# Two chained norms between the blocks: both sums from one pass, and fused norm bodies

## The reference

```python
h = h + swiglu(rmsnorm(h, norm2_w[layer]), w_ffn_in[layer], w_ffn_out[layer])
return rmsnorm(h, final_norm_w)
```

```python
h_l = rms_norm(x_lat, g_norm_mix[i]) * (1.0 + sc1_l) + sh1_l
```

## Time and profile before

| what | value |
|---|---|
| median of 3 runs | 3028.16 us (3027.71 to 3032.05) |
| the profiled execution | 3027.03 us, its span 3025.2 us |
| TensorE busy | 2884.8 us, 95% |
| VectorE, ScalarE, GpSimd busy | 1829.3, 1187.3, 305.2 us |
| mean granted TensorE clock | 0.984 of full speed |

### The profile page before, as it was taken

The page is one execution under the profiler, slowest core; times in us unless marked ns, Lnnn a source line. Parts: engine busy times, 40 slices in busy tenths (PEclk is TensorE's granted clock), DMA queues, the critical chain, the costliest instruction groups (busy, mean ns, idle before and its releaser), DMA issues.

```text
span 3025.2 us, 43358 instructions
## 1 busy us (share of the span) xinstructions
PE 2884.8 (95%) x18438; PEld 2347.4 (78%) x18438; DVE 1829.3 (60%) x2548; ACT 1187.3 (39%) x1667; POOL 305.2 (10%) x284
## 2 busy tenths in 40 slices
PE   8999888998999999999999999998999999998999
PEld 7888888997864788877657887875678887774899
DVE  4477766555456466664875677556646775546454
ACT  3245564445234422234244222344442223425443
POOL 1000001101000201112011111200120011000110
PEclk9999999999999999999999999999999999998999
DMA  8836324454211244432113444330034443211353
GB/s 294 332 132 238 126 84 168 170 189 159 98 42 42 91 188 153 183 138 99 69 43 139 153 181 167 125 109 29 16 139 165 171 179 112 99 70 42 140 181 126
DMA packets 59617, 407.01 MB, mean 135 GB/s; under 512 B 6520, under 2 KB 9848, under 8 KB 11168
## 3 DMA queue, kind: packets, MB, share of 16 engines
q1 hardware_dynamic: 58224, 400.00, 36.1%
q0 software_dynamic: 1200, 4.23, 0.5%
HBM read 402.60 MB, written 1.09 MB: 133 GB/s over the span
## 4 chain that ended last, share of the span: by engine, by line
PE 83%; DVE 8%; ACT 5%; issue 2%; POOL 0%; DMA 0%; DVEq 0%; ACTq 0%
PE bank L600 25%; PE bank L602 24%; PE bank L601 24%; DVE wlo L1970 3%; ACT whi L1336 2%; PE bank L1089 1%; ACT part L1593 1%; PE bank L1139 1%; PE bank L1214 1%; PE bank L1083 1%; PE bank L700 1%; PE bank L1093 1%; ACT xnhi L1596 1%; PE bank L1230 1%; PE bank L724 0%
## 5 line engine op out<-in xcount | busy, mean ns | idle before, releaser
L1970 DVE TENSOR_TENSOR wlo<-raw,whi 128x2048 fp32r<-128x2048 f32 x281 | 647.3, 2304 | 457.4 <-ACT whi L1336 457.3
L1336 ACT CAST whi<-raw 128x2048 fp32r<-128x2048 f32 x281 | 535.3, 1905 | 617.8 <-PE bank L602 612.1
L600 PE MATMUL bank<-xnhi,whi 128*128 128x512 f32 (+1 forms) x1760 | 663.6, 377 | 39.2 <-DVE xnlo L2383 18.8
L602 PE MATMUL bank<-xnhi,wlo 128*128 128x512 f32 (+1 forms) x1760 | 649.6, 369 | 0.0
L601 PE MATMUL bank<-xnlo,whi 128*128 128x512 f32 (+1 forms) x1760 | 647.8, 368 | 0.0
L600 PEld LDWEIGHTS bank<-xnhi,whi 128*128 128x128 f32 x1760 | 336.0, 191 | 136.7 <-issue 59.9
L602 PEld LDWEIGHTS bank<-xnhi,wlo 128*128 128x128 f32 x1760 | 336.1, 191 | 57.0
L601 PEld LDWEIGHTS bank<-xnlo,whi 128*128 128x128 f32 x1760 | 336.6, 191 | 53.8 <-issue 0.2
L600 PE MATMUL bank<-hidhi,whi 128*128 128x512 f32 (+1 forms) x1024 | 373.3, 365 | 0.0
L601 PE MATMUL bank<-hidlo,whi 128*128 128x512 f32 (+1 forms) x1024 | 372.4, 364 | 0.0
L602 PE MATMUL bank<-hidhi,wlo 128*128 128x512 f32 (+1 forms) x1024 | 372.1, 363 | 0.0
(11 more groups left out here) (328 smaller groups left out, 4058.9 us busy)
## 6 DMA issues: line engine op xcount, KB each, us to landing
raw<-in_wall SPq DMA_DIRECT2D x317, 1024.0 KB, 4.8
vraw<-in_wall SPq DMA_DIRECT2D x60, 1024.0 KB, 4.8
x<-in_x SPq DMA_DIRECT2D x2, 1024.0 KB, 6.8
bias<-relative_offsets POOLq DMA_DIRECT2D x2, 768.0 KB, 7.2
x<-relative_offsets POOLq DMA_DIRECT2D x2, 768.0 KB, 9.7
out<-x SPq DMA_DIRECT2D x1, 1024.0 KB, 4.8
vec<-in_vec SPq DMA_DIRECT2D x1, 665.0 KB, 10.0
aqk<-aqk POOLq DMA_DIRECT2D x2, 256.0 KB, 3.3
```

Of the source, the lines that this page charges most:

```text
L600: mm(out, wh, xh, start=first, stop=False)
L602: return mm(out, wl, xh, start=False, stop=last)
L1336: nc.scalar.copy(b.whi[u % SPL][:], b.raw[pos % RAW][:]).then_inc(*R.made("hi_ready"))
L1970: ttn(b.wlo[u % SPL][:], b.raw[blocks[u] % RAW][:], b.whi[u % SPL][:], ALU.subtract).then_inc(*R.made("lo_ready"))
```

## The change

Both norms' sums are made in one pass. While the last four units add to `x`, ScalarE makes two squares of each token chunk: of `x` (left half of `part`) and of `x` times the closing norm's weight (right half, L1577 and L1578 of the new file). GpSimd adds them 512 wide, TensorE sums them by `norm_sum`. With r the inverse root of the first sum's mean, the second norm's sum is the right half times r squared: ScalarE makes Ln and two Exps, VectorE multiplies (L2388), ScalarE makes Ln and Exp again, VectorE multiplies the two roots (L2404). The closing norm's weight goes into the first conditioned norm's scale (`scales`). `x` itself is written only after the norm's body (L2430).

The context's squares are made in the middle pass of the feed-forward, one per unit, added on GpSimd and summed by one product behind that pass; the table load and the context's root stand in the last pass, ahead of the four units out.

In all eight conditioned norms the scale goes into VectorE's product (L2418, once per stream), ScalarE adds only the shift and writes `xnhi` at once (L1623), and VectorE adds the shift again in the subtraction (L2409, once per stream).

```diff
-
-    def column_sums(t):
-
-        pe.wait_ge(*R.next("stat_read"))
-        g["norms"] += 1
-        for c in range(KC):
-            pe.wait_ge(*R.next("square_ready"))
-            mm(bank[4][:, 0:t], ones, b.part[c % 4][:, 0:t], start=(c == 0), stop=(c == KC - 1)) \
-                .then_inc(*R.made("first_summed" if c < KC - 1 else "sum_ready"))
...
     for p, n in enumerate((8, 8, 6)):
         stage(n, b.xn1, S, fresh=(p == 0))
         stage(4, b.big, S, kc=n, fresh=True)
-    norm_sum(S)
+        if p == 1:
+            pe.wait_ge(R.sems["ctx_summed"], KC - 1)
+            mm(bank[6][:, 0:S], ones, b.part[2][:, S:T2], start=True, stop=True).then_inc(*R.made("ctx_sum_ready"))
...
@@ -1289,12 +1282,7 @@
             return
         m = which * GAPM
         block = lambda n=1: mods(i + 1, n, bank[5], m)
-        if i == 0 and which == 0:
-            keep_on(3, bank[7])
-            column_sums(t)
-            block()
-        else:
-            norm_sum(t, within=block)
+        norm_sum(t, within=block)
         keep_on(2, bank[7])
         block()
         for k in first_units(b.xn, tokens, **kw):
...
-    for n in (8, 8, 6):
+    def ctx_square(c):
+
+        if c == 0:
+            act.wait_ge(R.sems["ctx_loaded"], 16)
+        if c >= 2:
+            act.wait_ge(R.sems["ctx_summed"], max(1, c - 2))
+        fn(b.part[c % 2][:, S:T2], b.x[:, c, S:T2], ACT.Square).then_inc(*R.made("ctx_square"))
+
+    def final_squares(k):
+
+        for c in range(2 * k, 2 * k + 2):
+            R.n["evac"] += 1
+            act.wait_ge(R.sems["chunk_taken"], R.value("evac"))
+            if c == 2 or c >= 4:
+                act.wait_ge(*R.next("square_summed"))
+            w = VEC["final"][0] + c
+            fn(b.part[c % 2][:, 0:S], b.x[:, c, 0:S], ACT.Square)
+            fn(b.part[c % 2][:, S:T2], b.x[:, c, 0:S], ACT.Square, scale=b.vec[:, w:w + 1]) \
+                .then_inc(*R.made("square_ready"))
+
+    def stat(dst, src):
+        fn(dst, src, ACT.Ln, bias=b.small[:, 63:64], scale=1.0 / D).then_inc(*R.made("act_step"))
+        act.wait_ge(*R.own("act_step"))
+
+    for p, n in enumerate((8, 8, 6)):
         def ffn(k):
             chunk()
             room()
             fn(b.sg[0][:, 0:S], bank_of(0)[:, 0:S], ACT.Sigmoid).then_inc(*R.made("gate_ready"))
             R.n["evac"] += 1
             part(b.big[0][:, k, :], width=S, by_chunk=R.value("evac"))
+            if p == 1:
+                ctx_square(k)
         stage(n, ffn)
-        stage(4, taken_squares(S) if n == 6 else None)
-    tables()
-    rstd(S, D, ahead=False)
+        if p == 2:
+            tables()
+            act.wait_ge(R.sems["ctx_sum_ready"], 1)
+            ctx = b.rstd[:, S:T2]
+            stat(ctx, bank[6][:, 0:S])
+            fn(ctx, ctx, ACT.Exp, scale=-0.5)
+        stage(4, final_squares if p == 2 else None)
+    R.next("square_summed")
+    split()
+    log = b.sg[1][:, 0:S]
+    act.wait_ge(*R.next("sum_ready"))
+    stat(log, bank[4][:, 0:S])
+    fn(b.sg[1][:, S:T2], log, ACT.Exp, scale=-1.0).then_inc(*R.made("final_inverse"))
+    fn(b.sg[0][:, 0:S], log, ACT.Exp, scale=-0.5)
+    R.made("stat_read")
+    act.wait_ge(*R.own("stat_read"))
+    second = b.sg[0][:, S:T2]
+    stat(second, second)
+    fn(second, second, ACT.Exp, scale=-0.5).then_inc(*R.made("rstd_ready"))
...
@@ -1589,11 +1619,9 @@
             act.wait_ge(*R.next("part_ready"))
             p = b.part[g["part"] % 4]
             for s in range(t // S):
-                o, sc, sh = s * S, 2 * (which * KC + c) + s, 2 * (3 * which * KC + c) + s
-                fn(p[:, o:o + S], p[:, o:o + S], ACT.Identity, scale=b.modg[i % 2][:, sc:sc + 1],
-                   bias=b.mod[i % 2][:, sh:sh + 1]).then_inc(*R.made("act_step"))
-            act.wait_ge(*R.own("act_step"))
-            nc.scalar.copy(b.xn[0][:, c, 0:t], p[:, 0:t]).then_inc(*R.made("part_hi"))
+                o, sh = s * S, 2 * (3 * which * KC + c) + s
+                last = fn(b.xn[0][:, c, o:o + S], p[:, o:o + S], ACT.Identity, bias=b.mod[i % 2][:, sh:sh + 1])
+            last.then_inc(*R.made("part_hi"))
             g["part"] += 1
...
@@ -1803,18 +1831,7 @@
 
     for i in range(LAYERS):
         t = S if i == LAYERS - 1 else T2
-        if i == 0:
-            act.wait_ge(R.sems["ctx_loaded"], 16)
-            act.wait_ge(R.sems["part_lo"], R.value("m part_hi"))
-            for c in range(KC):
-                act.wait_ge(*R.next("norm_input"))
-                if c >= 4:
-                    act.wait_ge(*R.next("first_summed"))
-                fn(b.part[c % 4][:], b.x[:, c, :], ACT.Square).then_inc(*R.made("square_ready"))
-            R.next("first_summed", 3)
-            split()
-            rstd_of(T2, D)
-        else:
+        if i:
             rstd(T2, D)
         operand_parts(i, 0, T2)
...
-    for n in (8, 8, 6):
-        parts(n, b.big, S)
-    sum_squares(S)
+    for p, n in enumerate((8, 8, 6)):
+        for c in range(n):
+            part(b.big[0][:, c, 0:S], b.big[1][:, c, 0:S], width=S)
+            if p == 1 and c:
+                total = b.part[2][:, S:T2]
+                pool.wait_ge(R.sems["ctx_square"], c + 1)
+                if c > 1:
+                    pool.wait_ge(*R.own("ctx_summed"))
+                tt(total, b.part[c % 2][:, S:T2], b.part[0][:, S:T2] if c == 1 else total, ALU.add) \
+                    .then_inc(*R.made("ctx_summed"))
     for i in range(LAYERS):
         t = S if i == LAYERS - 1 else T2
-        if i == 0:
-            R.next("square_ready", KC)
-        else:
-            sum_squares(T2)
+        sum_squares(T2)
         parts_elsewhere(KC)
...
         stage(4, add_to_x)
-    norm1("final", b.x)
-    dve.wait_ge(*R.own("norm_input"))
+    scales = b.small[:, 48:48 + KC]
+    step(ttn(scales, b.modg[0][:, 0:2 * KC].rearrange("p (c s) -> p c s", s=2)[:, :, 0], vec("final", 0, KC), ALU.mult))
+    dve.wait_ge(R.sems["final_inverse"], 1)
+    ttn(b.sg[0][:, S:T2], bank[4][:, S:T2], b.sg[1][:, S:T2], ALU.mult).then_inc(*R.made("stat_read"))
...
         ahead = i < LAYERS - 1
         pairs = paired(i, which)
         dve.wait_ge(*R.next("rstd_ready"))
+        if i == 0 and which == 0:
+            step(ttn(b.rstd[:, 0:S], b.sg[0][:, 0:S], b.sg[0][:, S:T2], ALU.mult))
 
         def second_half(c):
             dve.wait_ge(R.sems["part_hi"], first + c + 1)
-            ttn(b.xn[1][:, c, 0:t], b.part[(first + c) % 4][:, 0:t], b.xn[0][:, c, 0:t], ALU.subtract) \
-                .then_inc(*R.made("part_lo"))
+            for s, o in streams(t):
+                last = stt(b.xn[1][:, c, o:o + S], b.part[(first + c) % 4][:, o:o + S], mcol(i, 3 * which, c, s),
+                           b.xn[0][:, c, o:o + S], ALU.add, ALU.subtract)
+            last.then_inc(*R.made("part_lo"))
         first = g["part"]
         for c in range(KC):
-            ttn(part(t), b.x[:, c, 0:t], b.rstd[:, 0:t], ALU.mult).then_inc(*R.made("part_ready"))
+            p = part(t)
+            for s, o in streams(t):
+                sc = 2 * (which * KC + c) + s
+                scale = scales[:, c:c + 1] if i == 0 and which == 0 and s == 0 else b.modg[i % 2][:, sc:sc + 1]
+                last = stt(p[:, o:o + S], b.x[:, c, o:o + S], scale, b.rstd[:, o:o + S], ALU.mult, ALU.mult)
+            last.then_inc(*R.made("part_ready"))
             if pairs and c == 2:
                 second_half(0)
                 split()
@@ -2393,6 +2425,11 @@
         if pairs:
             second_half(KC - 2)
         second_half(KC - 1)
+        if i == 0 and which == 0:
+            for c in range(KC):
+                stt(b.x[:, c, 0:S], b.x[:, c, 0:S], vec("final", c), b.sg[0][:, 0:S], ALU.mult, ALU.mult) \
+                    .then_inc(*R.made("norm_input"))
+            dve.wait_ge(*R.own("norm_input"))
         if ahead:
             take_rows(bank[5])
             take_mods(i + 1, which * GAPM, GAPM, bank[5])
```

More of the change, by code:

```diff
@@ L174 @@
 SEMS = (["raw_loaded%d" % i for i in range(RAW)] + [
-    "first_loaded", "params_loaded", "tables_loaded", "x_loaded", "ctx_loaded", "first_summed", "rel_table", "rel_stored", "rel_loaded0", "rel_loaded1", "wg2_loaded",
+    "ctx_square", "ctx_summed", "ctx_sum_ready", "final_inverse", "first_loaded", "params_loaded", "tables_loaded", "x_loaded", "ctx_loaded", "first_summed", "rel_table", "rel_stored", "rel_loaded0", "rel_loaded1", "wg2_loaded",
     "rope_loaded", "keys_swapped", "result_ready", "stored",
```

## The result

The changed kernel takes **3035.64 us** (median of 15 runs, 3030.04 to 3040.92), the kernel before beside it on the same chip 3030.24 (15 runs, 3026.05 to 3035.55): ratio **1.0019**, 95% interval 1.0011 to 1.0027, so 3.3 to 8.2 us more. In a later comparison the same kernel gave 1.0012 (1.0003 to 1.0021), 0.9 to 6.4 us more. Both ratios lie within the bound of 0.2%, so this is the forecast's no change, on the slow side and inside its range. The profiled execution took 3030.88, its span 3029.0.

A forecast was written before the change was run, and what follows sets the result against it. The chain of waits, 83% TensorE, was taken as the bound, with a ScalarE-VectorE loop in the first block's last four units. Terms 0.45 + 2.1 + 2.6 - 6.7 + 0.4 - 1.4 + 3.1 + 2.5 gave +3.1: 3031.3 us, range 3025.5 to 3037.5.

The forecast's parts named there:

- Context's squares: Middle feed-forward stage: eight squares on ScalarE delay `whi` by 0.33 us each, within 0.6 of room; 0, at most 2.6.
- Context's product: TensorE, context's sum: the product has no gap to go into, half of a 512-wide one; +0.45 us.
- Table load and root: ScalarE, before the loop stage's second `whi`: load, logarithm and exponential for the context, no longer hidden; +2.1 us.
- Doubled squares: Loop stage: two more ScalarE activations per unit, 0.88 us, counting in three of four units; +2.6 us (2.0 to 3.0).
- Last adds to first `part`: First block's norms: the first `part` starts 8.8 us after the adds instead of 15.5; -6.7 us at full clock.
- Write of `x`: Eight VectorE writes now ahead of `modrow`, for which TensorE waits; +3.1 us, with a wait of 5 us or more.
- Clock behind `modrow`: TensorE at 1.2 GHz after gaps: 1.4 us in the sums, most of another drop behind `modrow`; +2.5 together (0 to 7).
- Norm bodies: All eight norms: two-stream bodies about a tie, last layer's first norm perhaps 0.3 us later; together +0.4 (-1.5 to +1.5).
- last norm: One-stream last norm: body takes 8.1 us, VectorE alone needs 6.7; -1.4 us.
- slow rival: Loop stage: clock stays down, 36 products last 8.5 us instead of 4.2; 3037.5 us; chance of over 3034.2: 0.29.
- faster rival: Table load absorbed, clock kind: 3023.9 us, or 3020.8 with `x`'s write off TensorE's path; chance of under 3022.1: 0.08.
- handed-over steps: Six steps behind the first norm's sum: 0.5 us each; a rival had 1, giving 3034 us, chance 0.1.

The follow-up runs named there:

- e4_root_late: Changed kernel with the table load and the context's root moved behind the last squares, instead of ahead of the second `whi`; ratio 1.0000 to the kernel before.
- e6_keep_on: Changed kernel with four unread products of ones in each of TensorE's three gaps in the first norm; ratio 0.9993 to the kernel before.
- e3_x_late: Changed kernel with the eight writes of `x` behind the copy `modrow` and the conditioning rows, not ahead of them; ratio 0.9987 to the kernel before.
- e5_squares_late: Changed kernel with the last pass's squares behind the split of the next unit but one; ratio 1.0000 to the kernel before.
- e7_all: Changed kernel with late squares, table load and context's root behind the squares, and writes of `x` behind `modrow`; ratio 0.9975 to the kernel before.

## Why the prediction came out, step by step

The forecast was +3.1 us, no change on the slow side. By the local stretches the change is worth +0.9 (context's squares and product, ahead of A), +4.1 to +4.3 (A+B+C), about -0.1 (the six other norms with two streams, medians of ten profiles against four) and -2.1 to -2.4 (last norm, up to the third unit): **+2.4 to +3.0**.

- *Context's squares, 0:* wrong by +0.4 to +0.5. The cover for `whi` was smaller than the 0.6 us that I had counted: TensorE's units grew to 5.68 and 5.75 us, which I had named as a sign of being wrong, and its products start 0.22 apart instead of 0.12 at 612.32, right behind the end of a `wlo` (612.26).
- *Context's product, +0.45:* right; the four units with it take 23.85 us in the changed kernel instead of 23.42 (next unit: unchanged).
- *Table load and root, +2.1:* 2.24, and e4_root_late gives 2.21 back. The instruction behind the load starts 1.29 us after it (704.86 to 706.15), as in the earlier trace rows. The Trainium skill (ScalarE: Activation LUTs, What ACT_TABLE_LOAD costs) has a drain of about 1.4 us with each load that switches sets; by that the term would have been 3.5. The trace doesn't show it: 23 of its 32 loads have the next ScalarE instruction 1.29 us behind their start.
- *Doubled squares, +2.6:* 0.76, 0.77 and 0.90, 2.4 in all. The third is larger because `wlo` itself took 2.43 instead of 2.29.
- *Last adds to first `part`, -6.7 and +1.4 for the clock:* -5.2 and, in the second profile, -5.1. e6_keep_on shows the share of the clock as 1.46.
- *Write of `x`, +3.1:* first `part` to `modrow` grew by 3.13. e3_x_late removes it whole. But TensorE's wait for `modrow` was 3.63 us, and 3.06 in the second profile, not the 5 or more that I had named as a sign. TensorE came late to it: the gap of 3.77 us ahead of the body had brought a drop (0.51 from 742 to 745), which the body on VectorE hid.
- *Clock behind `modrow`, +1.1 (the rest of the +2.5):* 1.57 and 1.22. Right in kind, up to half a microsecond short.
- *Norm bodies, +0.4, and last norm, -1.4:* mis-sized. An ordinary norm gains 0.15 at best, because VectorE no longer waits for the last casts; the last layer's first norm loses 0.2 (I had 0.3), and the six together come to about -0.1 instead of +0.4. The last norm's body is 1.7 shorter (16.11 to 14.45 us between `wlo` starts), and 0.5 to 0.8 more comes in the two units behind it, which the sum had left out.

So the mechanism was right at the large terms. The misses partly cancel, and that is luck: the bodies with the last norm came out 1.2 to 1.5 us better than forecast, the context's squares 0.4 to 0.5 and the clock behind `modrow` up to 0.5 worse. The local +2.4 to +3.0 lies in the second measured interval (0.9 to 6.4 us) and just below the first (3.3 to 8.2). For each of the other ten edited kernels the local sum, made in the same way, lies in its interval. **Open** is whether the changed kernel loses another microsecond or two somewhere by chance of the clock or whether the first comparison lay high. Its first profile shows one such place, ahead of everything that was edited: one unit took 7.05 us instead of 5.24, at half the full clock from 499.7 to 506.5; the second profile doesn't have it.

*The rivals.* The slow rival was right that the clock falls in the loop stage and wrong on what it costs: the granted clock is 0.57 from 711 to 715, behind the gap of 2.90 us, but the turns are 6.00, 6.02 and 6.14, so the longer products stayed hidden in the loop, and the slow case's 8.5 appeared nowhere. The Trainium skill (TensorE: Matmul & The Clock Gate, Why this matters for your kernels) warns against idle gaps between bursts of matmuls above a certain length, which bring half the rate. Here length alone didn't decide: gaps of 2.41 us ahead of the sum brought a drop in both profiles of the kernel before, 2.79 did in one profile and not in another (e6_keep_on, e3_x_late), and 2.94 ahead of L713 brought none (e5_squares_late). The gaps of 4.25 to 4.42 us ahead of the sum (seven profiles) and of 3.06 to 3.63 ahead of L713 (four) all brought a stretch at 1.2 GHz, worth 1.2 to 2.8 us. The faster rival needed the root absorbed, which it was not, and the write off TensorE's path, which only e3_x_late did. The handed-over steps cost about 0.5 us each, not 1 (736.81 to 739.74: six steps in 2.93 us).

## What to carry to other kernels

Shortening a chain pays only if the work taken out of it lands where an engine waits anyway: here 5.2 us were won in the norm and 4.7 spent in a loop just ahead of it, plus 4.7 because eight writes that nobody needed yet stood ahead of one copy that TensorE was waiting for. In an in-order queue, put the small thing that another engine awaits first, and ask of each stage whether weights are split a unit ahead or in a loop with the result. Where a gap of TensorE ahead of a short, serial chain can't be closed, a few products into an unused bank are worth as much as 2.7 us, but only if they end before the awaited operand is there.

## What the runs showed that I had not expected

**The same program takes two times in a stretch with short gaps.** Between 400 and 431 us, which no edit touches, two units take 30.6 us in some executions and 34.8 in others. The kernel before, and the same kernel in its second profile, in windows of 3 us (columns as above):

```profile
403.00:406.00 3.00, 1.75 (x22) 1.58 (x23) 2.97 (x7) 1.29 (x3) 0.00 (x0) 1.00 0.83 295
406.00:409.00 3.00, 3.00 (x34) 2.69 (x32) 1.32 (x4) 1.77 (x6) 0.00 (x0) 1.00 0.15 60
```

```profile
404.00:407.00 3.00, 1.90 (x16) 1.63 (x16) 2.97 (x7) 1.14 (x3) 0.00 (x0) 0.55 0.83 314
407.00:410.00 3.00, 3.00 (x15) 2.94 (x14) 1.20 (x4) 0.00 (x0) 0.00 (x0) 0.50 0.09 36
```

TensorE had idled 2.7 us in both (from 401.5 and from 402.4 on), and only in the second was 1.2 GHz granted behind it: 15 products instead of 34 in 3 us. Over the 14 profiles the first 508 us of the kernel before (61 units) take 492.5 to 492.9 us five times, 494.5 once and 496.5 to 497.6 eight times, in kernels old and new alike. Stretches with two such times also lie between 2690 and 2800 us. One of them alone is 4.2 us of the 4 to 13 us by which the 6 to 15 runs of one kernel differ. A change of a few microseconds is therefore read from local stretches of more than one profile.

**VectorE's `wlo` and GpSimd's 512-wide adds hold each other up:** the one that starts second pays. Where `wlo` starts while an add runs, it takes 2.43 us instead of 2.29 (720.93 in the changed kernel, 0.27 us before an add's end) and 2.81 (722.97 in e7_all, 0.66 us before one). Where an add starts while `wlo` runs, it ends 1.1 to 1.2 us behind `wlo`'s end, whatever its start: in e7_all such adds took 1.98, 2.69 and 3.13 us, against 1.26 to 1.30 for the others. GpSimd's times are the roughest of the profile.
